# Six loads of the modulation rows move from the input projection to the output projection, and the shift row is finished one chunk later

## Chip, cores and metric

The kernel runs on one core of a Trainium2 chip. The metric is the device time of one execution in microseconds (us). Before the change the median of three runs is 2752.85 us (2752.37 to 2753.55).

## What is computed

Two transformer blocks over 256 tokens of width 2048. What matters here is the first one's modulation: a conditioning vector `c` is multiplied with a 2048 x 12288 matrix, and the result is cut into six rows of 2048.

```python
mod = c_act @ w_ada[l] + b_ada[l]
sh_m, sc_m, gt_m, sh_f, sc_f, gt_f = jnp.split(mod[:, None, :], N_MOD, axis=-1)
h = rmsnorm(x, pre_mix_norm[l]) * (1.0 + sc_m) + sh_m
proj = h @ w_in[l]
...
y = jnp.concatenate([o_hg, o_gdn], axis=-1) @ w_out[l]
x = x + gt_m * rmsnorm(y, post_mix_norm[l])
h = rmsnorm(x, pre_ffn_norm[l]) * (1.0 + sc_f) + sh_f
y = jnp.square(jax.nn.relu(h @ w_ff1[l])) @ w_ff2[l]
x = x + gt_f * rmsnorm(y, post_ffn_norm[l])
```

`gt_m`, `sh_f` and `sc_f` are needed only after the output projection (`@ w_out`), `gt_f` at the end of the block.

## The kernel before

**Units, pairs and chunks.** Every large product is a list of chunks. A chunk is 1024 columns of a weight matrix with all rows of the contraction, which are taken 128 at a time: a *unit*. For one unit ScalarE (ACT) copies the weights to a rounded high part (L424), VectorE (DVE) subtracts that to get a low part (L437), and TensorE (PE) runs twelve matmuls of 512 columns (L475 to L477). Four units may be prepared ahead of the one in work. Weights arrive two units at a time: one DMA of 1 MiB, a *pair*, issued by SyncE (SP, L363) into a ring of four buffers. A load waits until the one four places earlier in the list has been used, so the ring holds whatever the next four loads of the list are. In a chunk of 16 units the pairs are numbered 0 to 7.

**Loads of the modulation rows.** `w_ada` is streamed through the same ring. A chunk's table `ada` names the pairs after which such a load stands in the list (`ada_after`, `load_of`). Each is again 1 MiB: 256 rows of the matrix by half a modulation row of 1024 columns, named by half row (0 to 7) and row pair (0 to 7). DVE uses it after the low part of the pair's second unit, in two steps of 128x1024 (`ada_step`, L455) which add into `MOD`. Half rows 0 and 1 are `gt_m`, 2 and 3 are the shift row `sh_f`; the scale row `sc_f` comes as 16 loads of whole rows after pair 1 of the output projection's first chunk (`mid`), and half rows 6 and 7 are `gt_f`. `ada_used` counts the steps.

**Stages around the change.** The input projection has a short first chunk and six whole ones, at 145 to 460 us of the profile. Its six whole chunks carry all 32 loads of half rows 0 to 3. The output projection (`mix1`, two chunks, *A* and *B* below) starts its units at once, but PE first works off the recurrent mixers (to about 628 us) in a hook of chunk A. From 630 to 732 us PE runs the 32 units of A and B.

**Summing a row.** The steps leave partial sums on each of the 128 partitions. `pe_mod_sum` (L1944) adds them up: eight matmuls with a table of ones into banks 4 to 7 (L1951), then one instruction copies the row back, for `gt_m` on DVE (`dve_mod0`, L2045), for the shift row on ACT (`act_mod1`, L2049), for the scale row on DVE (`dve_mod2`, L2054). All three stand in chunk A, before its units 9, 11 and 13. `dve_mod0` also waits for two rows of 2048 gains, which GpSimd (POOL) loads.

**The order on the engines.** Each engine takes its instructions strictly in order. DVE's list is, unit after unit: low part, the two steps of a modulation load if one stands after this pair, an evacuation of the chunk before, and the hook of the unit two places back. In chunk B that evacuation stands at unit 2: ACT squares a bank, which serves as scratch banks 4 and 5 (L696), DVE multiplies it with `gt_m` (L569), and that frees the bank for PE's first matmul of chunk B.

**POOL's loads.** Once PE has turned the second half of the mixers' output (before unit 7 of chunk A), `pool_norm_ffn1` issues, without waiting in between, two rows spread over all partitions (1 MiB each), the stored memory rows (2 MiB), `x` (2 MiB) and two small ones (L1934 to L1937, L1836). They go through POOL's queue (q0), SP's loads through q1, both on the same 16 DMA engines.

Of the kernel before, what the change touches and what calls it, by code (L numbers as in the profile page):

```python
# [20 lines left out]
KT = D // 128  # L21
# [14 lines left out]
UW = 1024  # L36
# [14 lines left out]
class Chunk:  # L51
# [16 lines left out]
    def ada_after(self, j):  # L68


        return self.mid * (j == 1) if self.mid else int(bool(self.ada) and j in self.ada)

# [9 lines left out]
def number(segments, first_loads, mod_sums, first_out):  # L82
# [5 lines left out]
    ada = 0  # L88
    for iters, chunks in segments:
        for i in range(iters):  # L90
            for c in chunks:
                now = dict(u=u, n=n, ada=ada, done=list(done), signals=list(signals), prev=(prev or {}).get("end"))
                for k in range(0, c.kn, 2):
                    u += min(2, c.kn - k)
                    rel[n] = ("lo", u)
                    n += 1
                    for _ in c.fill if k // 2 == FILL_AFTER else ():
                        native += 1
                        rel[n] = ("native", native)
                        n += 1  # L100
                    for _ in range(c.ada_after(k // 2)):
                        ada += 1 if c.mid else 2
                        rel[n] = ("ada", ada)
                        n += 1
# [57 lines left out]
def block_pair(nc, a, out, stop=None):  # L162

    with ExitStack() as ctx:
# [117 lines left out]
        for n, j in enumerate((6, 7, 0, 1, 2, 3)):  # L282
            for x in ((1, 2, 3, 5, 7), (1, 2, 3, 5, 6, 7))[n >= 4]:
                in_ada.setdefault(j, {})[x] = divmod(sum(len(y) for y in in_ada.values()), 8)
# [11 lines left out]
                          for r0, kn, ph in ((0, 10, "w_out_ab"), (1280, 6, "w_out_c")) for h in range(2)])],  # L296
# [9 lines left out]
                           (1, down2(5, phase="hid2_last", lhs=second))]  # L306
        stages["ffn1"][-1][1][1].phase = "ffn1_tail"
        stages["co"][0][1][1].phase = "co_tail"
        stages["mix2"][0][1][-1].phase = "mix2_tail"
# [29 lines left out]
        if stop != "in":  # L339
            segs[in_segs][1][0].mid = KT  # L340
            segs[in_segs][1][1].ada = mod_loads(6, 0, 1, 3, 5, 7)
        RELEASE, TAIL = number(segs, FIRST_LOADS, DVE_SUMS, ("copy", P, 4 * UW, 0))


# [8 lines left out]
        def sp_chunk(sp, c, i):  # L353
# [12 lines left out]
            for k in range(0, c.kn, 2):  # L366
# [24 lines left out]
                for x in range(c.ada_after(k // 2)):  # L391
                    if c.mid:
                        load(RAW[:, n % RAWN, :, :].rearrange("p j n -> p (j n)"),
                             a["w_ada"][x * 128:x * 128 + 128, 4 * D:5 * D])
                        continue
                    half_row, q = c.ada[k // 2]
                    x0 = 2 * D + half_row * UW
                    load(RAW[:, n % RAWN, :, :], a["w_ada"][q * 256:q * 256 + 256, x0:x0 + UW].rearrange(
                        "(j p) n -> p j n", p=128))
# [30 lines left out]
        def dve_chunk(dve, c, i, hooks, evac):  # L430

            for k in range(c.kn):
# [6 lines left out]
                if c.ada and k % 2 == 1 and k // 2 in c.ada:  # L439
# [4 lines left out]
                    for j in range(2):  # L444
                        ada_step(dve, acc, RAW[:, m % RAWN, j, :], 2 * pair + j,
                                 c.at["ada"] + 2 * sum(c.ada_after(x) for x in range(k // 2)) + j)
                if k == c.dve_evac:
# [95 lines left out]
        def act_evac(act, c, i):  # L543
# [15 lines left out]
            for b, t, h, w, count, (sem, value), col in out_banks(c, i, ("post",)):  # L559
                act.wait_ge(sem, value)  # L560
                act.wait_ge(S("mod_copied"), 3)
                act_square(act, "post_mix", b + 4 * (col // UW), PS[:, b, 0:w], PARTS["post_mix"][:, t, col // 512 + h:col // 512 + h + 1])
# [1076 lines left out]
        MIX1 = next(c for _, cs in segs for c in cs if c.phase == "mix1")  # L1639
        ADA_IN = 4 * KT  # L1640
        MIX_LOAD = MIX1.fill_load(len(KEY_FILL))
# [300 lines left out]

        def pe_mod_sum(pe, row, steps):

            pe.wait_ge(S("ada_used"), steps)
            if row:
                pe.wait_ge(S("mod_copied"), row)
            else:
# [84 lines left out]
        def pe_mod2(pe):  # L2033
            pe_mod_sum(pe, 2, ADA_IN + KT)

        def pe_mod0(pe):
            pe_mod_sum(pe, 0, ADA_IN)

        def pe_mod1(pe):
            pe_mod_sum(pe, 1, ADA_IN)  # L2040

# [5 lines left out]
        def act_mod1(act):  # L2047
            act.wait_ge(S("mod_summed"), 2)
            act.activation(MOD[:, 1, :], bank_cols(4, 4), ACT.Copy).then_inc(S("mod_copied"), 1)  # L2049

        def dve_mod2(dve):
            dve.wait_ge(S("mod_summed"), 3)
            dve.wait_ge(S("masks_in"), 48)
# [3 lines left out]
        def residual_ffn1(dve, link):  # L2057
            dve.wait_ge(S("x2_in"), 16)
            dve_residual(dve, link, "post_mix", Y)

# [87 lines left out]
        def pe_ffn1_tail(pe):  # L2148
            pe_mod_sum(pe, 3, ADA_IN + 3 * KT)

# [835 lines left out]
        def wait_hidden(pe, c, i):  # L2986
            if c.w is a["w_ff2"]:
                wait_hid(pe, c, i)
            else:
# [11 lines left out]
                  ("in1_last", dict(pe=[None] * 10 + [pe_in1_last])),  # L3001
                  ("mix1", dict(pe=tile_waits("mix1", (0, pe_mix1), (7, pe_gdn_split), (9, pe_mod0), (11, pe_mod1), (13, pe_mod2)),
                                act=[None, act_mix1] + [None] * 4 + [act_gdn_split] + [None] * 4 + [act_mod1],
                                dve=[None, dve_mix1, dve_gdn_scale, dve_gdn_gate] + [None] * 2 + [dve_gdn_split] + [None] * 2 +
                                [dve_mod0] + [None] * 3 + [dve_mod2])),
                  ("norm_ffn1", norm_ffn1),
# [135 lines left out]
```

## Time and profile before

| | us |
|---|---|
| median of three runs | 2752.85 |
| the profiled execution | 2751.32 |
| its span, first to last instruction | 2749.5 |
| PE busy | 2663.8 (97%) |
| DVE busy | 1785.1 (65%) |
| ACT busy | 1225.0 (45%) |

The profile is one execution; all stretches below are its times from the start of the span. The rest of the execution's own time, 1.8 us, lies outside the span. A matmul's row says 0.39 us, but such matmuls are pipelined and start about 0.227 us apart, so a unit of twelve takes 2.72 us, and a gap in PE's work is read from the starts and from the idle time in brackets behind a row. A DMA's time to landing counts from its issue on the queue to its completion.

### The profile page before, as it was taken

What the parts mean: (1) busy time and instruction counts of PE and PEld (TensorE: products, weight loads), DVE (VectorE), ACT (ScalarE), POOL (GpSimd) and SP (SyncE); (2) the same over time, 40 slices, a digit from 0 to 9 for tenths busy, and PEclk for the clock granted to TensorE, in tenths of its full rate; (3) what the DMA queues carried; (4) which work ended last, traced back from release to release, by engine and by line L of the source; (5) the groups of instructions that cost most, each with busy time, mean ns of one, the idle gap of its engine ahead of it and who ended that gap; (6) DMA issues with size and microseconds to landing.
All of it is one profiled execution on the core that took longest, in us unless ns stands there. A gap on an engine that the chain in (4) does not pass through costs nothing.

```text
span 2749.5 us, 32675 instructions
## 1 busy us (share of the span) xinstructions
PE 2663.8 (97%) x12618; PEld 2163.5 (79%) x12618; DVE 1785.1 (65%) x2178; ACT 1225.0 (45%) x1572; POOL 69.3 (3%) x92
## 2 busy tenths in 40 slices
PE   5899999899999999999999999999999999999998
PEld 3478887687888888888887777788888888888896
DVE  7887677995785555555577355667665565656576
ACT  2155645343444444444344355544654434353443
POOL 1000000001000000000000100000000000000000
PEclk9999999999999999999999999999999999999999
DMA  9988887345595555555574544444455555555553
GB/s 376 370 289 273 297 303 267 138 178 212 200 365 186 187 191 187 183 189 191 184 290 162 192 154 146 139 160 161 161 199 184 191 188 188 183 186 180 199 173 118
DMA packets 166944, 571.73 MB, mean 208 GB/s; under 512 B 9993, under 2 KB 30648, under 8 KB 162609
## 3 DMA queue, kind: packets, MB, share of 16 engines
q1 hardware_dynamic: 161936, 544.25, 57.3%
q0 software_dynamic: 4720, 25.57, 2.5%
q8 instruction: 74, 1.21, 0.2%
q10 hardware_dynamic: 176, 0.40, 0.0%
q14 instruction: 38, 0.30, 0.0%
HBM read 562.58 MB, written 7.60 MB: 207 GB/s over the span
## 4 chain that ended last, share of the span: by engine, by line
PE 61%; issue 28%; DVE 7%; DMA 2%; ACT 2%; POOL 0%; SPq 0%; DVEq 0%; POOLq 0%; ACTq 0%
PE banks L475 17%; PE banks L477 17%; PE banks L476 17%; DMA raw_weights<-in_w_ada 2%; PE banks L592 1%; DVE mod_in L1019 1%; PE banks L932 1%; ACT weights_high L424 1%; DVE proj L1231 1%; DVE weights_low L437 1%; PE banks L893 1%; PE banks L1951 0%; DVE proj L1215 0%; DMA first_weights<-in_w_in 0%; PE banks L1153 0%
## 5 line engine op out<-in xcount | busy, mean ns | idle before, releaser
L437 DVE TENSOR_TENSOR weights_low<-raw_weights,weights_high 128x1024 fp32r<-128x1024 f32 (+2 forms) x814 | 967.3, 1197 | 732.4 <-ACT weights_high L424 725.0
L424 ACT ACTIVATE weights_high<-raw_weights 128x1024 fp32r<-128x1024 f32 (+2 forms) x814 | 838.8, 1037 | 930.7 <-PE banks L477 889.4
L475 PE MATMUL banks<-weights_high,lhs_high 128*128 128x512 f32 (+1 forms) x2264 | 899.1, 397 | 7.8 <-DVE lhs_low L605 2.2
L477 PE MATMUL banks<-weights_high,lhs_low 128*128 128x512 f32 (+1 forms) x2264 | 882.1, 390 | 0.0
L476 PE MATMUL banks<-weights_low,lhs_high 128*128 128x512 f32 (+1 forms) x2264 | 880.6, 389 | 0.0
L475 PEld LDWEIGHTS banks<-weights_high,lhs_high 128*128 128x128 f32 x2264 | 426.6, 188 | 101.0 <-issue 8.6
L477 PEld LDWEIGHTS banks<-weights_high,lhs_low 128*128 128x128 f32 x2264 | 426.0, 188 | 88.4
L476 PEld LDWEIGHTS banks<-weights_low,lhs_high 128*128 128x128 f32 x2264 | 427.0, 189 | 82.4 <-issue 1.2
L475 PE MATMUL banks<-weights_high,hid_high 128*128 128x512 f32 x768 | 300.8, 392 | 3.0 <-DVE y_rows L574 1.7
L477 PE MATMUL banks<-weights_high,hid_low 128*128 128x512 f32 x768 | 299.2, 390 | 0.0
L476 PE MATMUL banks<-weights_low,hid_high 128*128 128x512 f32 x768 | 299.1, 389 | 0.0
L475 PEld LDWEIGHTS banks<-weights_high,hid_high 128*128 128x128 f32 x768 | 144.2, 188 | 37.2 <-DVE y_rows L574 4.3
L477 PEld LDWEIGHTS banks<-weights_high,hid_low 128*128 128x128 f32 x768 | 144.2, 188 | 30.1
L476 PEld LDWEIGHTS banks<-weights_low,hid_high 128*128 128x128 f32 x768 | 144.2, 188 | 29.3
L455 DVE SCALAR_TENSOR_TENSOR modulation<-raw_weights,columns,modulation 128x1024 f32<-128x1024 f32 (+1 forms) x112 | 160.7, 1434 | 2.6
L1019 DVE SCALAR_TENSOR_TENSOR mod_in<-raw_weights,columns,mod_in 128x512 f32<-128x512 f32 (+1 forms) x150 | 95.5, 645 | 12.3 <-DMA raw_weights<-in_w_ada 7.0
L932 PE MATMUL banks<-first_weights,x_turned 128*128 128x512 f32 x192 | 90.1, 630 | 7.3 <-ACT x_turned L971 6.3
L932 PEld LDWEIGHTS banks<-first_weights,x_turned 128*128 128x128 f32 x192 | 38.3, 202 | 55.3 <-issue 48.7
L2902 ACT ACTIVATE modulation<-modulation 128x512 f32<-128x512 f32 (+1 forms) x22 | 13.7, 623 | 105.6 <-DVE modulation L2929 105.6
L475 PE MATMUL banks<-weights_high,proj_turned 128*128 128x512 f32 x128 | 51.6, 404 | 2.9 <-DVE proj_turned L2530 1.3
L476 PE MATMUL banks<-weights_low,proj_turned 128*128 128x512 f32 x128 | 51.0, 398 | 0.0
L477 PE MATMUL banks<-weights_high,proj_turned 128*128 128x512 f32 x128 | 50.0, 391 | 0.0
(429 smaller groups left out, 2070.0 us busy)
## 6 DMA issues: line engine op xcount, KB each, us to landing
raw_weights<-in_w_ff SPq DMA_DIRECT2D x128, 1024.0 KB, 4.9
raw_weights<-in_w_ada SPq DMA_DIRECT2D x96, 1024.0 KB, 6.9
raw_weights<-in_w_in SPq DMA_DIRECT2D x96, 1024.0 KB, 5.4
raw_weights<-in_w_up SPq DMA_DIRECT2D x80, 1024.0 KB, 5.0
raw_weights<-in_w_down SPq DMA_DIRECT2D x42, 1024.0 KB, 5.0
raw_weights<-in_w_out SPq DMA_DIRECT2D x32, 1024.0 KB, 5.1
first_weights<-in_w_in SPq DMA_DIRECT2D x16, 768.0 KB, 11.9
raw_weights<-in_w_up SPq DMA_DIRECT2D x16, 384.0 KB, 3.8
```

Of the source, the lines that this page charges most:

```text
L424: act.activation(WHI[:, u % SPN, 0:c.width], raw_unit(c, n, k), ACT.Copy).then_inc(S("high_made"), 1)
L437: dve.tensor_tensor(WLO[:, u % SPN, 0:c.width], raw_unit(c, n, k), WHI[:, u % SPN, 0:c.width].bitcast(F32), ALU.subtract).then_inc(S("low_ ...
L455: dve.scalar_tensor_tensor(out=acc, in0=row, scalar=COLS[:, 112 + kt:113 + kt], in1=acc, op0=ALU.mult, op1=ALU.add).then_inc(S("ada_used"), 1)
L475: nc.tensor.matmul(o, x, hi, start=(k == 0), stop=False)
L476: nc.tensor.matmul(o, x, lo, start=False, stop=False)
L477: mm = nc.tensor.matmul(o, y, hi, start=False, stop=(k == c.kn - 1))
L592: tr = nc.tensor.transpose(bank[:, k, 128 * t:128 * t + 128], rows[:, t, c0:c0 + 128], IDENT)
L893: mm = nc.tensor.matmul(PS[:, 6 + t, 0:256], x[:, 128 * t:128 * t + 128], w, start=(k == 0), stop=(k == KT - 1))
L932: mm = nc.tensor.matmul(PS[:, bank, :], XTURN[:, k, 128 * t:128 * t + 128], raw[:, 512 * h:512 * h + 512], start=(k == 0), stop=(k == KT - 1))
L1019: ins = dve.scalar_tensor_tensor(out=acc, in0=row, scalar=c, in1=acc, op0=ALU.mult, op1=ALU.add)
L1231: dve.copy_predicated(self.at[:, t, :].rearrange("p (h n) -> p h n", h=H), mask, self.slot(t).rearrange("p (h n) -> p h n", h=H)).then_inc ...
L2902: act.activation(dst[:, 2 * q:2 * q + nk, :], GT[:, 2 * q:2 * q + nk, :], func).then_inc(S(done), 1)
```

## The change

Six of the 32 loads leave the input projection: its six whole chunks now carry 4, 4, 4, 4, 5 and 5 loads in place of 5, 5, 5, 5, 6 and 6, and half of half row 3 is missing at its end. Four of the six follow pairs 4 to 7 of chunk A, two follow pairs 1 and 2 of chunk B, whose own four loads of `gt_f` move from pairs 1, 3, 5, 7 to 3, 5, 6, 7. The shift row is so complete only in chunk B: its sum on PE and its copy on ACT move there, to unit 10. The scale row's sum moves from unit 13 of A to unit 12 and becomes the second. The waits on the counts follow.

```diff
     def ada_after(self, j):
-        return self.mid * (j == 1) if self.mid else int(bool(self.ada) and j in self.ada)
+        return self.mid * (j == 1) + int(bool(self.ada) and j in self.ada)
...
         for n, j in enumerate((6, 7, 0, 1, 2, 3)):
-            for x in ((1, 2, 3, 5, 7), (1, 2, 3, 5, 6, 7))[n >= 4]:
+            for x in ((1, 3, 5, 7), (1, 2, 4, 5, 7))[n >= 4]:
                 in_ada.setdefault(j, {})[x] = divmod(sum(len(y) for y in in_ada.values()), 8)
...
+        stages["mix1"][0][1][1].phase = "mix1_end"
...
             segs[in_segs][1][0].mid = KT
-            segs[in_segs][1][1].ada = mod_loads(6, 0, 1, 3, 5, 7)
+            segs[in_segs][1][0].ada = {4: (3, 2), 5: (3, 3), 6: (3, 4), 7: (3, 5)}
+            segs[in_segs][1][1].ada = {1: (3, 6), 2: (3, 7), **mod_loads(6, 0, 3, 5, 6, 7)}
...
                 act.wait_ge(sem, value)
-                act.wait_ge(S("mod_copied"), 3)
+                act.wait_ge(S("mod_copied"), 2 + col // UW)
                 act_square(act, "post_mix", b + 4 * (col // UW), ...
...
-        ADA_IN = 4 * KT
+        ADA_IN = 52
...
         def pe_mod2(pe):
-            pe_mod_sum(pe, 2, ADA_IN + KT)
+            pe_mod_sum(pe, 2, ADA_IN + KT, 1)
         def pe_mod0(pe):
-            pe_mod_sum(pe, 0, ADA_IN)
+            pe_mod_sum(pe, 0, 2 * KT, 0)
         def pe_mod1(pe):
-            pe_mod_sum(pe, 1, ADA_IN)
+            pe.wait_ge(S("squares_summed"), SQUARES_BEFORE["post_mix"] + 4)
+            pe_mod_sum(pe, 1, 5 * KT, 2)
...
         def residual_ffn1(dve, link):
             dve.wait_ge(S("x2_in"), 16)
+            dve.wait_ge(S("mod_copied"), 3)
...
-                  ("mix1", dict(pe=tile_waits("mix1", (0, pe_mix1), (7, pe_gdn_split), (9, pe_mod0), (11, pe_mod1), (13, pe_mod2)),
-                                act=[None, act_mix1] + [None] * 4 + [act_gdn_split] + [None] * 4 + [act_mod1],
+                  ("mix1", dict(pe=tile_waits("mix1", (0, pe_mix1), (7, pe_gdn_split), (9, pe_mod0), (12, pe_mod2)),
+                                act=[None, act_mix1] + [None] * 4 + [act_gdn_split],
                                 dve=[None, dve_mix1, dve_gdn_scale, dve_gdn_gate] + [None] * 2 + [dve_gdn_split] + [None] * 2 +
-                                [dve_mod0] + [None] * 3 + [dve_mod2])),
+                                [dve_mod0] + [None] * 2 + [dve_mod2])),
+                  ("mix1_end", dict(pe=[None] * 10 + [pe_mod1], act=[None] * 10 + [act_mod1])),
```

Two places show what this does to the order. The first is SP's list of loads from the scale row on; `in_w_out` are the pairs of the output projection, `in_w_ada` 128x2x1024 the half-row loads. Before:

```order
111 L363 DMA raw_weights<-in_w_ada 128x2048 x16
112 L363 DMA raw_weights<-in_w_out 128x2x1024 x8
113 L363 DMA raw_weights<-in_w_ada 128x2x1024
114 L363 DMA raw_weights<-in_w_out 128x2x1024 x2
115 L363 DMA raw_weights<-in_w_ada 128x2x1024
```

With the change:

```order
99 L365 DMA raw_weights<-in_w_ada 128x2048 x16
100 L365 DMA raw_weights<-in_w_out 128x2x1024 x3
101 L365 DMA raw_weights<-in_w_ada 128x2x1024
102 L365 DMA raw_weights<-in_w_out 128x2x1024
103 L365 DMA raw_weights<-in_w_ada 128x2x1024
104 L365 DMA raw_weights<-in_w_out 128x2x1024
105 L365 DMA raw_weights<-in_w_ada 128x2x1024
106 L365 DMA raw_weights<-in_w_out 128x2x1024
107 L365 DMA raw_weights<-in_w_ada 128x2x1024
108 L365 DMA raw_weights<-in_w_out 128x2x1024 x2
109 L365 DMA raw_weights<-in_w_ada 128x2x1024
110 L365 DMA raw_weights<-in_w_out 128x2x1024
```

The eight pairs (2 to 7 of chunk A, 0 and 1 of chunk B) stood in one run; now a half-row load stands behind each of pairs 4 to 7.

The second is DVE's list in chunk A from unit 9 on, to the evacuation in chunk B. Before, from the low parts of units 9 to 11:

```order
306 L437 TENSOR_TENSOR weights_low<-raw_weights,weights_high 128x1024 x3
307 L2045 TENSOR_TENSOR modulation<-banks,vec 128x2048
308 L437 TENSOR_TENSOR weights_low<-raw_weights,weights_high 128x1024 x4
309 L2054 SCALAR_TENSOR_TENSOR modulation<-banks,hid_rows 128x2048
310 L437 TENSOR_TENSOR weights_low<-raw_weights,weights_high 128x1024 x3
311 L569 TENSOR_TENSOR y_rows<-banks,modulation 128x512 x4
```

With the change, from the steps behind unit 9:

```order
295 L457 SCALAR_TENSOR_TENSOR modulation<-raw_weights,columns,modulation 128x1024 x2
296 L439 TENSOR_TENSOR weights_low<-raw_weights,weights_high 128x1024 x2
297 L457 SCALAR_TENSOR_TENSOR modulation<-raw_weights,columns,modulation 128x1024 x2
298 L2048 TENSOR_TENSOR modulation<-banks,vec 128x2048
299 L439 TENSOR_TENSOR weights_low<-raw_weights,weights_high 128x1024 x2
300 L457 SCALAR_TENSOR_TENSOR modulation<-raw_weights,columns,modulation 128x1024 x2
301 L439 TENSOR_TENSOR weights_low<-raw_weights,weights_high 128x1024
302 L2057 SCALAR_TENSOR_TENSOR modulation<-banks,hid_rows 128x2048
303 L439 TENSOR_TENSOR weights_low<-raw_weights,weights_high 128x1024
304 L457 SCALAR_TENSOR_TENSOR modulation<-raw_weights,columns,modulation 128x1024 x2
305 L439 TENSOR_TENSOR weights_low<-raw_weights,weights_high 128x1024 x3
306 L571 TENSOR_TENSOR y_rows<-banks,modulation 128x512 x4
```

The low parts of units 10 to 15 and the row copies now stand between pairs of steps, each of which needs its own load to have landed.

## Rows read from the trace of the kernel before

**Rows 1.** Page, part 1 and the second row of part 2.

```profile
PE 2663.8 (97%) x12618; PEld 2163.5 (79%) x12618; DVE 1785.1 (65%) x2178; ACT 1225.0 (45%) x1572; POOL 69.3 (3%) x92
```

**Rows 2.** Stretches of the input projection; columns as the first row says.

```profile
core 0: us, PE busy (x) PEld busy (x) DVE busy (x) ACT busy (x) POOL busy (x), PEclk, DMA share, GB/s
...
200.00:320.00 120.00, 120.00 (x590) 99.69 (x589) 90.68 (x108) 78.98 (x99) 2.64 (x3) 1.00 0.84 295
335.00:459.00 124.00, 124.00 (x567) 103.14 (x566) 91.94 (x80) 52.86 (x57) 1.81 (x1) 1.00 0.87 304
```

**Rows 3.** PE's waits from 145 to 461 us: total us, times, longest.

```profile
PE banks L877 <- ACT proj L556: 0.9, 1, 0.9
PE banks L475 <- ACT proj L556: 0.4, 1, 0.4
```

**Rows 4.** More stretches: slow clock in the input projection, and around waits of PE.

```profile
321.00:324.50 3.50, 3.50 (x11) 2.76 (x11) 0.47 (x1) 0.00 (x0) 0.00 (x0) 0.52 1.01 360
331.40:334.80 3.40, 3.40 (x11) 2.82 (x11) 0.27 (x1) 0.27 (x1) 0.00 (x0) 0.50 1.02 357
...
1553.30:1556.80 3.50, 3.50 (x10) 2.74 (x9) 0.00 (x0) 0.20 (x1) 0.61 (x2) 0.51 0.99 380
466.00:474.00 8.00, 6.34 (x34) 4.08 (x33) 7.08 (x23) 7.17 (x11) 0.00 (x0) 1.00 0.41 148
```

**Rows 5.** PE in order of time: the row sums of chunk A; start us, us, instruction.

```profile
658.56 3.59 PE L1951 MATMUL banks<-modulation,tables 128*128 128x512 f32 x8
661.59 0.79 PE L475 MATMUL banks<-weights_high,lhs_high 128*128 128x512 f32 x1
...
667.45 3.59 PE L1951 MATMUL banks<-modulation,tables 128*128 128x512 f32 x8
670.48 0.79 PE L475 MATMUL banks<-weights_high,lhs_high 128*128 128x512 f32 x1
```

**Rows 6.** PE in order of time: first matmul of chunk B; idle before it in brackets.

```profile
688.55 0.47 PE L475 MATMUL banks<-weights_high,lhs_high 128*128 128x512 f32 x1 [0.44 <-DVE y_rows L569]
```

**Rows 7.** SP's issues in order of time, 644 to 692 us.

```profile
644.99 13.98 SPq L363 DMA_DIRECT2D raw_weights<-in_w_out  x4
668.06 0.37 SPq L363 DMA_DIRECT2D raw_weights<-in_w_ada  x1
676.33 9.15 SPq L363 DMA_DIRECT2D raw_weights<-in_w_out  x2
```

**Rows 8.** DMA issues 653.8 to 657.5 us: KB each, us to landing.

```profile
memory_here<-memory_turned POOLq DMA_DIRECT2D x1, 2048.0 KB, 14.8
x_rows<-in_x POOLq DMA_DIRECT2D x1, 2048.0 KB, 22.5
...
hid_rows<-in_pre_ffn_norm POOLq DMA_DIRECT2D x1, 1024.0 KB, 9.0
raw_weights<-in_w_out SPq DMA_DIRECT2D x1, 1024.0 KB, 15.5
```

**Rows 9.** DMA issue at 658.6 us.

```profile
raw_weights<-in_w_out SPq DMA_DIRECT2D x1, 1024.0 KB, 21.7
```

**Rows 10.** DMA issue at 668.1 us.

```profile
raw_weights<-in_w_ada SPq DMA_DIRECT2D x1, 1024.0 KB, 15.4
```

**Rows 11.** DMA queues from 670 to 672 us: packets, MB, share of the engines.

```profile
q1 hardware_dynamic: 66, 0.24, 30.6%
q0 software_dynamic: 65, 0.53, 66.0%
```

**Rows 12.** DVE in order of time, 655 to 692 us.

```profile
655.09 3.50 DVE L437 TENSOR_TENSOR weights_low<-raw_weights,weights_high 128x1024 fp32r<-128x1024 f32 x3
663.47 2.29 DVE L2045 TENSOR_TENSOR modulation<-banks,vec 128x2048 f32<-128x2048 f32 x1 [4.89 <-DMA hid_rows<-in_pre_ffn_norm]
665.68 2.35 DVE L437 TENSOR_TENSOR weights_low<-raw_weights,weights_high 128x1024 fp32r<-128x1024 f32 x2
...
687.72 2.48 DVE L569 TENSOR_TENSOR y_rows<-banks,modulation 128x512 f32<-128x512 f32 x4
...
691.57 2.60 DVE L455 SCALAR_TENSOR_TENSOR modulation<-raw_weights,columns,modulation 128x1024 f32<-128x1024 f32 x2
```

**Rows 13.** ACT in order of time: high parts of chunk B while PE never waits.

```profile
694.37 1.06 ACT L424 ACTIVATE weights_high<-raw_weights 128x1024 fp32r<-128x1024 f32 x1 [1.66 <-PE banks L477]
697.09 1.06 ACT L424 ACTIVATE weights_high<-raw_weights 128x1024 fp32r<-128x1024 f32 x1 [1.66 <-PE banks L477]
```

**Rows 14.** PE in order of time: the wait ahead of the slow clock at 1553 us.

```profile
1552.06 0.91 PE L2316 MATMUL banks<-modulation 33*128 33x384 f32 x2 [2.05 <-ACT modulation L2456]
```

More of the change, by code:

```diff
@@ L101, in number @@
                     for _ in range(c.ada_after(k // 2)):
-                        ada += 1 if c.mid else 2
+                        ada += 1 if c.mid and k // 2 == 1 else 2
                         rel[n] = ("ada", ada)
@@ L391, in sp_chunk @@
                 for x in range(c.ada_after(k // 2)):
-                    if c.mid:
+                    if c.mid and k // 2 == 1:
                         load(RAW[:, n % RAWN, :, :].rearrange("p j n -> p (j n)"),
@@ L445, in dve_chunk @@
                         ada_step(dve, acc, RAW[:, m % RAWN, j, :], 2 * pair + j,
-                                 c.at["ada"] + 2 * sum(c.ada_after(x) for x in range(k // 2)) + j)
+                                 c.at["ada"] + 2 * sum(c.ada_after(x) for x in range(k // 2)) - (c.mid or 0) + j)
                 if k == c.dve_evac:
@@ L1941, in pool_norm_ffn1, with pe_mod_sum @@
             pool_store_values(pool, 0)
-        def pe_mod_sum(pe, row, steps):
+        def pe_mod_sum(pe, row, steps, copied):
             pe.wait_ge(S("ada_used"), steps)
-            if row:
-                pe.wait_ge(S("mod_copied"), row)
+            if copied:
+                pe.wait_ge(S("mod_copied"), copied)
             else:
@@ L2047, in act_mod1 @@
         def act_mod1(act):
-            act.wait_ge(S("mod_summed"), 2)
+            act.wait_ge(S("mod_summed"), 3)
             act.activation(MOD[:, 1, :], bank_cols(4, 4), ACT.Copy).then_inc(S("mod_copied"), 1)
         def dve_mod2(dve):
-            dve.wait_ge(S("mod_summed"), 3)
+            dve.wait_ge(S("mod_summed"), 2)
             dve.wait_ge(S("masks_in"), 48)
@@ L2148, in pe_ffn1_tail @@
         def pe_ffn1_tail(pe):
-            pe_mod_sum(pe, 3, ADA_IN + 3 * KT)
+            pe_mod_sum(pe, 3, 7 * KT, 3)
         def act_ffn1_tail(act):
```

## The prediction

> **What bounds the kernel.** The page's busy times come first: PE works 97% of the span [rows 1], so a change gains only where PE stands still, and costs wherever it makes PE stand still. The table by stretches then shows the stage from which loads are taken: between 200 and 320 us PE is busy 120.00 of 120.00 us, between 335 and 459 us 124.00 of 124.00 [rows 2], although the DMA engines are at 0.84 to 0.87. The list of PE's waits names 1.3 us in all from 145 to 461 us, both behind an evacuation by ACT and neither behind a load [rows 3]. The unit's pace is read from ACT's high parts, which follow PE's releases 2.72 us apart [rows 13]. So the input projection is bound by PE, and DVE and DMA lie beside it. In the output projection the order in time of PE, SP, DVE and the landings must be read together, because there POOL's loads come in. I count times as in the trace of before, and call the pairs of chunk A W5, W6, W7, those of chunk B V0, V1, and the four half-row loads of chunk A G1 to G4.
>
> **The input projection: 0 us.** It loses six loads of 1 MiB, and twelve steps at 1.3 us on DVE (two are 2.60 us [rows 12]). Both stood beside a PE that never waited for them. If this cover were gone, 12 x 1.3 = 15.6 us of DVE time would be the most to save; with PE busy throughout, the bound above is its 1.3 us of waits [rows 3]. Two stretches run at a granted clock of 0.52 and 0.50 [rows 4], 1.2 in place of 2.4 GHz, behind short matmuls; they cost 0.5 x (3.5 + 3.4) = 3.5 us, but the change touches nothing in front of them. I take 0, ends +1 and -4.8.
>
> **The row sums: moved, not saved.** The shift row's sum holds PE from 667.45 to 670.48 us, and the first matmul behind it takes 0.4 us longer than usual [rows 5]: 3.4 us. Before it stands in chunk A, afterwards in chunk B, so it is in the total both times. Its copy on ACT, and the waits put around it (the first four squares and the steps of chunk B's first two loads), end many units before PE's unit 10 of B; ACT, blocked on the sum behind its high part 12, has then prepared what PE needs next. I cost these waits at 0; the cover is the four prepared units, about 8 us (three of 2.72).
>
> **Chunk A: G1 to G4 take places in the ring.** Up to 656 us all goes as before: the ring then holds W4, G1, W5, G2 instead of W4 to W7. From there the loads meet POOL's. Before, SP issued V0 at 656.3 and V1 at 658.6 us as the ring came free [rows 7]; they took 15.5 and 21.7 us to land [rows 8, 9], so at 671.8 and 680.3. The next load, issued at 668.1, took 15.4 [rows 10] and landed at 683.5. The cause is in the same rows: POOL's memory rows and `x` (14.8 and 22.5 us [rows 8]) share the engines. Between 670 and 672 us the queues move 66 and 65 packets, but 0.24 against 0.53 MB [rows 11]: SP's queue gets a packet for each of POOL's, and a third of the bytes, as long as POOL's queue is full. Before, nothing suffered, since W6 and W7 were in the ring already.
>
> Afterwards the same places of SP's queue, issued at the same low parts, carry W6 and G3, then W7 and G4. So W6 lands at 671.8, G3 at 680.3, W7 at 683.5 us. Step by step:
> - PE without the shift row's sum passes units 9 to 11 and the scale row's sum by 673.2 (661.6 + 3 x 2.72 + 0.4 + 3.0). Unit 12 needs W6: high part 1.06 [rows 13], low part 1.15 (three take 3.50 [rows 12]), so 674.1: 0.9 us of waiting.
> - DVE does the low part of 13 and meets the steps of G3, which can't begin before 680.3; they take 2.6 us [rows 12]. W7 landed at 683.5, its high part ends at 684.5, the low part of unit 14 at 685.8. PE has finished unit 13 at 679.7 and waits 6.1 us.
> - DVE goes on without a gap: scale row 2.2 (as the `gt_m` row [rows 12]), low part 15 1.2, steps of G4 2.6, three low parts of chunk B 3.5: 695.3 us. Only then comes the evacuation that frees PE's first bank. Before, it began at 687.72 [rows 12] and PE's chunk B at 688.55 [rows 6], 0.83 us later; so afterwards chunk B begins at 696.1. V1, issued when G3 is used (682.9), lands at about 691, in time for this chain.
>
> Chunk B thus begins 7.5 us later and has the sum of 3.4 us still in it: **+10.9 us**. In chunk B DMA and DVE have caught up; each engine's pace is that of the input projection with modulation loads behind successive pairs, where PE never waited [rows 2]. The norm and the feed-forward follow directly on PE's end and move along.
>
> **The clock behind the new wait.** Before, PE waited 2.05 us at 1552 us [rows 14], behind narrow matmuls, and the granted clock was then 0.51 for a stretch of 3.5 us [rows 4], which costs 0.5 x 3.5 = 1.7 us. The new waits are 6.1 us, and some 4 us before chunk B. A slow stretch behind the first is hidden, since DVE sets the beginning of chunk B; one behind the second costs. Bounds 0 and 2 x 1.7; I take 1.7, since the new wait is longer than that of the row. The Trainium skill ("TensorE: Matmul & The Clock Gate", on the clock gate) says likewise that idling brings the slow clock back.
>
> **Sum.** 0 + 10.9 + 1.7 = 12.6 us. On the profiled execution's 2751.3 that is 2763.9; the median of the runs lies 1.5 us above that execution, which gives 2765.4, and I forecast **2765 us**. Bounds of the terms: from +4 (the waits half as long) to +17 (both slow stretches, and a further wait in chunk B).
>
> **Rivals.**
> - *Not slower: SP's queue catches up.* With three or four loads outstanding instead of two, SP could draw a larger part of the engines. The point from which it decides: G3 landed by about 668 and W7 by about 671 us. Then DVE's list from 663.5 us (row copy 2.2, two low parts, G3, low part, scale row, low part, G4, three low parts) ends near 684 us, as chunk A does on PE (673.2 + 4 x 2.72 = 684.1), and the price is 0: 2752.9 us. For it: SP's queue is merely shared, and DVE has room. Against: SP's queue never ran empty in this stretch before either, and still got 0.24 MB in 2 us [rows 11]; the landings are those of a full queue. The Trainium skill ("DMA: Bandwidth & Descriptors", section on queues, rings and completion order) states that an engine serves its queue rows in turn, a packet each. The 66 and 65 packets agree with it; by that rule more loads in one queue gain no larger part, and this rival gets 0.12 instead of an even chance.
> - *Half the price.* POOL's loads end earlier, or the waits overlap: chunk B begins 3 us earlier than worked out and the clock stays up: +6 to +8, 2760 us. 0.1.
> - *No slow clock:* +10.9, 2763.7 us. 0.2. For it: from 466 to 474 us PE was busy only 6.34 of 8.00 us, and the granted clock was 1.00 [rows 4].
> - *Worse:* a further wait in chunk B, where G loads follow pairs 1 and 2 at once, +14 to +17: 2768 us. 0.08.
> - *Faster.* Fewer loads in the input projection move its two slow stretches or end its waits: -4.8 at most, 2748 us, and the ring's trouble would have to stay away as well. 0.02 for more than 0.2%.
>
> **How the numbers follow.** The forecast itself has 0.48. About 0.2% (5.5 us) is what a measurement of this kernel can tell from no change. Slower by more: 0.48 + 0.2 + 0.08 + 0.1 = 0.86; within it 0.12; faster 0.02. The range 2757 to 2770 takes in all the slower cases and their bounds, and leaves out the other two, 0.14, and a little of the tails.
>
> **What would show it.** In the profile of the changed kernel: the input projection as before, PE without waits on loads; SP's loads issued between 656 and 664 us with 15 to 23 us to landing; DVE idle some 5 us before the steps of a G load near 680, released by a DMA; a PE wait of about 6 us behind a low part near 680 to 686, one of 3 to 4 us behind the evacuation near 692 to 696; the first matmul of chunk B at about 696 us, a slow-clock stretch behind it, and all later stages shifted by one amount. The prediction is wrong if W7 lands before 678 us, or if PE passes from A to B before 690.

## The result, and the profile after

| | before | after |
|---|---|---|
| median of six runs, us | 2752.89 | 2765.03 |
| lowest to highest, us | 2752.37 to 2753.55 | 2763.66 to 2766.93 |
| the profiled execution, us | 2751.32 | 2764.93 |
| its span, us | 2749.5 | 2763.1 |

The ratio is 1.0045, with a 95% interval of 1.0035 to 1.0055: the changed kernel is slower by 12.1 us, and the forecast was 2765. Lines are those of the changed kernel, two higher than before; those of an experiment are its own kernel's.

The page's busy times after the change answer to [rows 1]:

```profile
PE 2669.6 (97%) x12618; PEld 2166.2 (78%) x12618; DVE 1785.2 (65%) x2178; ACT 1224.7 (44%) x1572; POOL 69.3 (3%) x92
```

Every engine runs as many instructions as before, and only PE is busy longer, by 5.8 us: in the slow stretches its rows say 0.63 us for a matmul that takes 0.39 otherwise. The stretches of the input projection, and three at a low granted clock (columns as in [rows 2]):

```profile
200.00:320.00 120.00, 120.00 (x591) 99.66 (x588) 85.86 (x103) 78.91 (x99) 2.64 (x3) 1.00 0.82 278
335.00:459.00 124.00, 124.00 (x566) 103.08 (x566) 86.76 (x76) 52.64 (x56) 1.81 (x1) 1.00 0.82 285
683.30:690.10 6.80, 4.45 (x11) 3.51 (x12) 5.78 (x5) 3.68 (x4) 0.00 (x0) 0.50 0.89 342
697.00:700.30 3.30, 3.30 (x9) 2.62 (x8) 3.27 (x4) 0.47 (x1) 0.00 (x0) 0.50 0.78 226
1564.00:1570.70 6.70, 6.35 (x13) 4.30 (x14) 0.00 (x0) 1.17 (x3) 1.61 (x3) 0.50 0.73 245
```

DVE lost 4.8 and 5.2 us of work in the first two, the DMA engines 0.02 and 0.05 of their share, and PE was busy all the time, as in [rows 2]. Nothing was gained there: the `gt_m` row's sum starts at 658.77 us, where it started at 658.56 before [rows 5]. PE's waits from 655 to 750 us show where the time went:

```profile
PE banks L477 <- DVE weights_low L439: 6.1, 1, 6.1
PE banks L477 <- DVE y_rows L571: 2.1, 1, 2.1
PE banks L895 <- DMA raw_weights<-in_w_ckv: 0.3, 1, 0.3
```

The first two are the waits of the forecast, in front of unit 14 of chunk A and of chunk B. SP's issues at 656.5, 659.1, 661.3 and 663.8 us (W6, G3, W7, G4), each with its time to landing, and the queues from 670 to 672 us:

```profile
raw_weights<-in_w_out SPq DMA_DIRECT2D x1, 1024.0 KB, 14.8
...
raw_weights<-in_w_ada SPq DMA_DIRECT2D x1, 1024.0 KB, 20.9
...
raw_weights<-in_w_out SPq DMA_DIRECT2D x1, 1024.0 KB, 21.8
...
raw_weights<-in_w_ada SPq DMA_DIRECT2D x1, 1024.0 KB, 21.9
...
q0 software_dynamic: 63, 0.52, 65.6%
q1 hardware_dynamic: 65, 0.23, 29.6%
```

The four land at 671.3, 680.0, 683.1 and 685.7 us. With more loads outstanding SP's queue still gets a packet for each of POOL's and 0.23 of 0.75 MB, as in [rows 11]. The Trainium skill ("DMA: Bandwidth & Descriptors", section on queues, rings and completion order) gives the rule, an engine serving its queue rows in turn by packets; 65 against 63 packets agree with it.

DVE in order of time, then ACT, then PE:

```profile
663.74 2.28 DVE L2048 TENSOR_TENSOR modulation<-banks,vec 128x2048 f32<-128x2048 f32 x1
672.47 2.36 DVE L439 TENSOR_TENSOR weights_low<-raw_weights,weights_high 128x1024 fp32r<-128x1024 f32 x2 [6.45 <-ACT weights_high L426]
680.04 2.60 DVE L457 SCALAR_TENSOR_TENSOR modulation<-raw_weights,columns,modulation 128x1024 f32<-128x1024 f32 x2 [5.21 <-DMA raw_weights<-in_w_ada]
684.28 1.23 DVE L439 TENSOR_TENSOR weights_low<-raw_weights,weights_high 128x1024 fp32r<-128x1024 f32 x1 [1.64 <-ACT weights_high L426]
685.42 2.28 DVE L2057 SCALAR_TENSOR_TENSOR modulation<-banks,hid_rows 128x2048 f32<-128x2048 f32 x1
...
688.76 2.60 DVE L457 SCALAR_TENSOR_TENSOR modulation<-raw_weights,columns,modulation 128x1024 f32<-128x1024 f32 x2
691.27 3.49 DVE L439 TENSOR_TENSOR weights_low<-raw_weights,weights_high 128x1024 fp32r<-128x1024 f32 x3
694.68 2.47 DVE L571 TENSOR_TENSOR y_rows<-banks,modulation 128x512 f32<-128x512 f32 x4
```

```profile
671.38 2.01 ACT L426 ACTIVATE weights_high<-raw_weights 128x1024 fp32r<-128x1024 f32 x2 [14.01 <-DMA raw_weights<-in_w_out]
683.19 2.00 ACT L426 ACTIVATE weights_high<-raw_weights 128x1024 fp32r<-128x1024 f32 x2 [9.80 <-DMA raw_weights<-in_w_out]
```

```profile
658.77 3.59 PE L1953 MATMUL banks<-modulation,tables 128*128 128x512 f32 x8
...
670.38 3.59 PE L1953 MATMUL banks<-modulation,tables 128*128 128x512 f32 x8
673.84 0.47 PE L477 MATMUL banks<-weights_high,lhs_high 128*128 128x512 f32 x1
...
685.65 0.76 PE L477 MATMUL banks<-weights_high,lhs_high 128*128 128x512 f32 x1 [6.13 <-DVE weights_low L439]
...
693.05 0.39 PE L479 MATMUL banks<-weights_high,lhs_low 128*128 128x512 f32 x1
695.51 0.47 PE L477 MATMUL banks<-weights_high,lhs_high 128*128 128x512 f32 x1 [2.06 <-DVE y_rows L571]
...
724.43 3.59 PE L1953 MATMUL banks<-modulation,tables 128*128 128x512 f32 x8
...
744.66 3.69 PE L895 MATMUL banks<-raw_weights,memory_here 128*128 128x256 f32 x16 [0.30 <-DMA raw_weights<-in_w_ckv]
```

DVE stands idle 5.21 us until G3 has landed; ACT takes up W7 the moment it lands, at 683.19; from then to the evacuation at 694.68 DVE has no gap but 1.64 us. The shift row's sum stands in chunk B at 724.43. The last row is the first matmul of the norm's product, which follows chunk B. In the kernel before it is this one:

```profile
732.19 13.97 PE L893 MATMUL banks<-raw_weights,memory_here 128*128 128x256 f32 x64
```

From the start of the `gt_m` row's sum to this matmul PE needs 732.19 - 658.56 = 73.63 us before [rows 5] and 744.66 - 658.77 = 85.89 after: **12.26 us more, as much as the medians differ (12.1)**. This distance is used below as *the stretch*. It leaves out what an execution gains or loses earlier and later: the spans of the two profiled executions differ by 13.6 us, and of the other 1.3 us, 0.2 lie before it and the rest near 1564 us, where the slow stretch shown above is 6.7 us long and was 3.5 before [rows 4].

### The profile page after: what moved, and what is told of

Read it like the earlier page. It is cut to its first block, busy times and chain, and to the rows that moved or that the text cites. A ratio compares the mean times of both kernels' runs of the same rounds, so it can differ in the third digit from the quotient of the medians.

```text
span 2763.1 us, 32675 instructions
## 1 busy us (share of the span) xinstructions
PE 2669.6 (97%) x12618; PEld 2166.2 (78%) x12618; DVE 1785.2 (65%) x2178; ACT 1224.7 (44%) x1572; POOL 69.3 (3%) x92
## 4 chain that ended last, share of the span: by engine, by line
PE 60%; issue 28%; DVE 7%; DMA 3%; ACT 2%; POOL 0%; SPq 0%; DVEq 0%; POOLq 0%; ACTq 0%
PE banks L477 17%; PE banks L479 16%; PE banks L478 16%; DMA raw_weights<-in_w_ada 2%; PE banks L594 1%; DVE mod_in L1021 1%; PE banks L934 1%; PE banks L895 1%; ACT weights_high L426 1%; DMA raw_weights<-in_w_out 1%; DVE weights_low L439 1%; DVE modulation L457 1%; DVE proj L1233 1%; DVE proj L1217 0%; DMA first_weights<-in_w_in 0%
## 5 line engine op out<-in xcount | busy, mean ns | idle before, releaser
L1021 DVE SCALAR_TENSOR_TENSOR mod_in<-raw_weights,columns,mod_in 128x512 f32<-128x512 f32 (+1 forms) x150 | 95.5, 644 | 12.2 <-DMA raw_weights<-in_w_ada 6.8
```

Source lines behind the costliest of these rows:

```text
L1021: ins = dve.scalar_tensor_tensor(out=acc, in0=row, scalar=c, in1=acc, op0=ALU.mult, op1=ALU.add)
```

## The experiments

All times are medians; ratios are to runs of the kernel before on the same chip, whose medians were 2752.87 (e1 to e4), 2752.77 (e5 to e7) and 2752.45 us (e8 and e9).

| experiment | median, us | ratio, 95% interval | the stretch, us |
|---|---|---|---|
| before | 2752.89 | | 73.63 |
| after | 2765.03 | 1.0045 (1.0035 to 1.0055) | +12.26 |
| e3, only the sums moved | 2752.92 | 0.9999 (0.9989 to 1.0009) | -0.04 |
| e4, six loads left out | 2753.06 | 1.0001 (0.9992 to 1.0011) | -0.03 |
| e1, POOL's loads in pieces | 2762.71 | 1.0037 (1.0024 to 1.0050) | +7.30 |
| e2, the same in the kernel before | 2756.37 | 1.0009 (1.0000 to 1.0019) | -0.04 |
| e5, two loads in A, one behind pair 0 of B | 2762.03 | 1.0033 (1.0020 to 1.0045) | +6.61 |
| e6, none in A | 2755.82 | 1.0011 (1.0002 to 1.0021) | -0.01 |
| e7, POOL's pieces earlier | 2759.39 | 1.0023 (1.0013 to 1.0032) | +3.80 |
| e9, none in A, seven loads in B | 2752.57 | 1.0002 (0.9993 to 1.0011) | +0.36 |
| e8, none in A, eight loads in B | 2755.83 | 1.0012 (1.0003 to 1.0021) | +3.07 |

**e3: the kernel before, with only the sums moved.** The shift row's sum and copy go to unit 10 of B, the scale row's to unit 12 of A; all loads stay.

```diff
...
-... (9, pe_mod0), (11, pe_mod1), (13, pe_mod2)),
+... (9, pe_mod0), (12, pe_mod2)),
...
+("mix1_end", dict(pe=[None] * 10 + [pe_mod1], act=[None] * 10 + [act_mod1])),
...
```

> The kernel before with only the sum and the copy of the shift row moved to chunk B and the scale row's sum one unit earlier; all loads stay. Theory: PE runs the same instructions, and the waits put around the sum are met long before, so 2752.9 within 1 us. Rival (the sum's new place costs a part of the 12 us): 2756 or more.

2752.92 us, and the stretch is the same. The sums' new places and the waits around them cost nothing.

**e4: the kernel before without the six loads.**

```diff
-            for x in ((1, 2, 3, 5, 7), (1, 2, 3, 5, 6, 7))[n >= 4]:
+            for x in ((1, 3, 5, 7), (1, 2, 4, 5, 7))[n >= 4]:
...
-        ADA_IN = 4 * KT
+        ADA_IN = 52
```

> The kernel before with the input projection's 26 loads in their new places and the other six loads and their twelve steps left out altogether (the shift row lacks six of its sixteen parts). Theory: the input projection is bound by PE, so six loads and twelve steps less are worth nothing: 2752.9 within 1.5 us. Rival (the relief is worth something that the output projection then eats up): 2750 or less.

2753.06 us. The stretch from 200 to 320 us:

```profile
200.00:320.00 120.00, 120.00 (x590) 99.65 (x589) 85.86 (x103) 78.92 (x99) 2.64 (x3) 1.00 0.81 279
```

DVE is freed of 4.8 us and PE is as busy as ever: relieving the input projection of the six loads is worth nothing by itself.

**e1: the change, with POOL's memory rows and `x` in eight pieces of 512 KiB**, each issued behind a unit of chunk B instead of all at 655 us.

```diff
-            pool.dma_start(MEM_HERE[:, :, :].rearrange("p k t -> p (k t)"), a["memory_turned"]).then_inc(S("mem_in"), 16)
-            pool.dma_start(X[:, :, :], a["x"].rearrange("(t p) d -> p t d", p=128)).then_inc(S("x2_in"), 16)
+            last = stages["mix1"][0][1][1].at["u"]
+            for n, unit in enumerate((0, 1, 3, 5, 7, 9, 11, 13)):
+                pool.wait_ge(S("unit_used"), last + unit + 1)
...
```

> The changed kernel, but POOL's stored memory rows and x (2 MiB each) are issued in pieces of 512 KiB during chunk B instead of all at once before unit 7 of chunk A; every load and step of the change stays where it is. Theory (POOL's loads make SP's loads late): SP's loads issued at 656 to 664 us land in about 5 to 8 us, PE passes chunk A without the wait of 6 us and without a slow-clock stretch, chunk B begins near 685 us with the sum of 3.4 us still in it, and the median falls by most of the 12 us, to 2753 to 2757 (the rest for pieces that now meet chunk B's loads). Rival (the 10 us of steps on DVE, in order with the low parts, are too much for chunk A by themselves): the wait at unit 14 and at the start of chunk B stays, 2762 to 2766.

2762.71 us, far above what was expected. PE's waits from 640 to 745 us, and the four loads issued from 656 to 664 us:

```profile
PE banks L895 <- DMA raw_weights<-in_w_ckv: 7.2, 1, 7.2
PE banks L477 <- DVE weights_low L439: 1.0, 2, 0.5
PE banks L477 <- DVE y_rows L571: 0.4, 1, 0.4
```

```profile
raw_weights<-in_w_out SPq DMA_DIRECT2D x2, 1024.0 KB, 9.7
raw_weights<-in_w_ada SPq DMA_DIRECT2D x2, 1024.0 KB, 9.7
```

The mechanism is as the theory has it: without the two big transfers the same loads land in 9.7 us instead of 15 to 22 (5 to 8 were expected; POOL's two rows of 1 MiB are still beside them), the wait of 6.1 us is gone, and chunk B's wait is that of [rows 6]. But the transfers still have to be made. Their last pieces now meet the first loads of the norm's product. The one issued at 724.8 us:

```profile
raw_weights<-in_w_ckv SPq DMA_DIRECT2D x1, 1024.0 KB, 14.4
```

PE waits for it 7.2 us behind chunk B, and from 737.6 to 744.4 us the granted clock is 0.50: the norm's product takes 16.50 us instead of 13.97. With these 2.5 us, the stretch's 7.3 make the 9.8 by which the medians differ. The price was not removed but moved; the expectation had overlooked the next loads in SP's queue.

**e2: the kernel before, with the same pieces.** Same edit, in the kernel before.

> The kernel before with the same pacing of POOL's loads, to price the pacing alone. Theory: before, POOL's loads hid behind the full ring, so nothing is gained, and the pieces fit between chunk B's loads: 2752 to 2756. Rival (POOL's burst cost the kernel before something too): 2749 or less.

2756.37 us, just above what was expected. The stretch is unchanged; behind it PE loses 1.6 us in the norm, most of it in one wait of 2.3 us instead of 1.1. The rest of the 3.5 us was not located; the other delays of this execution lie near 136 us and from 1538 to 1563 us, in stretches of slow clock far from the edit. So these 1.6 us are what the trace shows as the price of spreading out POOL's loads alone. Whether it is more is not shown, and the interval begins at 1.0000.

**e7: as e1, but earlier.** POOL's two small loads go first, and the pieces follow units 0, 1, 2, 4, 6, 8, 10, 11 of B.

```diff
-            for n, unit in enumerate((0, 1, 3, 5, 7, 9, 11, 13)):
+            for n, unit in enumerate((0, 1, 2, 4, 6, 8, 10, 11)):
```

> The run with POOL's loads in pieces, with the two small scattered loads ahead of the pieces and the pieces earlier in chunk B, since the last pieces and the small loads made the first two weight loads of the memory values late there (a wait of 7.2 us after chunk B). All loads and steps of the change stay. Theory: no wait in chunk A, at most 2 us after chunk B: 2752 to 2756. Rival (the change costs its price somewhere whatever POOL does): 2760 or more.

2759.39 us, again above what was expected. PE's waits from 640 to 745 us, and the load issued at 726.0 us:

```profile
PE banks L895 <- DMA raw_weights<-in_w_ckv: 2.9, 1, 2.9
PE banks L477 <- DVE weights_low L439: 1.0, 2, 0.5
PE banks L477 <- DVE y_rows L571: 0.8, 1, 0.8
...
raw_weights<-in_w_ckv SPq DMA_DIRECT2D x1, 1024.0 KB, 10.0
```

The same load, which took 5.0 us before, now takes 10.0 and costs 2.9. Less, but not nothing: from 685 to 733 us the DMA engines' share is 1.00, against 0.77 before and 0.80 after the change. Chunk B has no free place for POOL's 4 MiB. The norm's product takes 15.59 us, again in part at a granted clock of 0.50; with these 1.6 us, the stretch's 3.8 make 5.4 of the 6.6 by which the medians differ.

**e5: two loads in chunk A instead of four**, behind pairs 4 and 5; the other four behind pairs 0 to 3 of B, the four of `gt_f` behind pairs 4 to 7.

```diff
-            segs[in_segs][1][0].ada = {4: (3, 2), 5: (3, 3), 6: (3, 4), 7: (3, 5)}
-            segs[in_segs][1][1].ada = {1: (3, 6), 2: (3, 7), **mod_loads(6, 0, 3, 5, 6, 7)}
+            segs[in_segs][1][0].ada = {4: (3, 2), 5: (3, 3)}
+            segs[in_segs][1][1].ada = {**mod_loads(3, 4, 0, 1, 2, 3), **mod_loads(6, 0, 4, 5, 6, 7)}
```

> The changed kernel with two of the four loads behind chunk A's pairs kept there (pairs 4 and 5) and two moved to chunk B, which carries shift loads behind pairs 0 to 3 and its own behind 4 to 7. Theory (what counts is which loads stand in SP's queue while POOL's burst holds the engines): W6 is still first in the queue and lands at about 671, W7 is now second and lands at about 680 in place of 683, DVE has no steps between units 13 and 14; PE waits about 3 us at unit 14 and chunk B begins near 689.5 in place of 695.5: +4 to +7, 2757 to 2760. Rival (four loads or two make no difference, the wait comes from the moved sum or the ring's two places): 2763 or more. Other rival (linear in the loads moved to A): half of 12, 2759, which does not tell it from the theory; the landing times do.

PE's waits from 640 to 745 us:

```profile
PE banks L477 <- DVE weights_low L439: 3.7, 3, 2.7
PE banks L477 <- DVE y_rows L571: 2.5, 1, 2.5
```

ACT takes up W7 when it lands, and DVE comes to the steps of the load behind pair 0 of B:

```profile
679.73 2.00 ACT L426 ACTIVATE weights_high<-raw_weights 128x1024 fp32r<-128x1024 f32 x2 [6.40 <-DMA raw_weights<-in_w_out]
687.56 2.60 DVE L457 SCALAR_TENSOR_TENSOR modulation<-raw_weights,columns,modulation 128x1024 f32<-128x1024 f32 x2
```

W7 now has the ring's place that G3 had and lands at 679.7 instead of 683.1 us. The wait in front of unit 14 is 2.7 instead of 6.1: shorter by about these 3.4 us. The load behind pair 0 puts its steps where those of G4 stood, so from W7's landing to chunk B's first matmul DVE has the same work as after the change. The stretch is 6.6 us longer, of which 3.2 stand in front of chunk B and 3.4 are the sum. The median, 2762.03 us, lies above what was expected. It is another 2.7 us higher than the stretch says, and 3.0 above the profiled execution (2758.99). Where the other runs lose this was not seen. Four of those five list a mean granted clock of 0.991, the profiled one 0.992; more slow clock would fit, but is not shown.

**e6: none in chunk A.** 28 loads stay in the input projection, four stand behind pairs 1 to 4 of B, and one of `gt_f`, for which B has no place left, goes to the feed-forward's first chunk. The shift row's sum stands at unit 12 of B.

```diff
-            segs[in_segs][1][0].ada = {4: (3, 2), 5: (3, 3), 6: (3, 4), 7: (3, 5)}
-            segs[in_segs][1][1].ada = {1: (3, 6), 2: (3, 7), **mod_loads(6, 0, 3, 5, 6, 7)}
+            segs[in_segs][1][1].ada = {**mod_loads(3, 4, 1, 2, 3, 4), **mod_loads(6, 0, 5, 6, 7)}
...
-... ada=mod_loads(6, 4, 3, 5, 6, 7)
+... ada={**mod_loads(6, 4, 3, 5, 6, 7), 2: (6, 3)}
```

> Four loads instead of six leave the input projection (28 stay there), and all four stand in chunk B, behind pairs 1 to 4; chunk B keeps three loads of its own, the fourth goes to the first chunk of the feed-forward; the shift row's sum stands at unit 12 of B. Nothing stands in chunk A's ring but its pairs, POOL's burst stays as it was. Theory: PE passes A without waits on loads, and B begins as early as before less the sum: 2752 to 2755. Rival (any load moved out of the input projection costs about 2 us where it goes): 2759 or more.

The stretch is as before: chunks A and B are free of new waits. The median, 2755.82 us, is 3.0 us above the kernel before and just above what was expected. What the profiled execution (the slowest of the ten) loses near the edit lies in the feed-forward, where the odd load stands. DVE there, then PE and a stretch at a low granted clock:

```profile
763.33 2.61 DVE L456 SCALAR_TENSOR_TENSOR modulation<-raw_weights,columns,modulation 128x1024 f32<-128x1024 f32 x2 [3.97 <-DMA raw_weights<-in_w_ada]
```

```profile
769.61 0.77 PE L476 MATMUL banks<-weights_high,lhs_high 128*128 128x512 f32 x1 [2.37 <-DVE weights_low L438]
769.20:772.60 3.40, 2.99 (x7) 2.47 (x8) 3.36 (x4) 1.58 (x2) 0.00 (x0) 0.50 1.02 376
```

It is the pattern of chunk A in small: steps that wait for their load hold up the low parts behind them. A new edit had brought a new wait, so the question was asked once more without it.

**e9: none in A, and only three loads moved.** 29 stay, three stand behind pairs 1 to 3 of B, the four of `gt_f` behind pairs 4 to 7. **e8: none in A, four moved.** 28 stay, and all eight pairs of B are followed by a load, pair 0 too.

```diff
...
+            segs[in_segs][1][1].ada = {**mod_loads(3, 5, 1, 2, 3), **mod_loads(6, 0, 4, 5, 6, 7)}    (e9)
...
+            segs[in_segs][1][1].ada = {**mod_loads(3, 4, 0, 1, 2, 3), **mod_loads(6, 0, 4, 5, 6, 7)} (e8)
...
```

> The change with 29 loads left in the input projection, none in chunk A, and three shift-row loads behind pairs 1 to 3 of chunk B, the four of gt_f behind pairs 4 to 7 (seven of eight pairs followed by a load); the sum and copy of the shift row stay in unit 10 of B. Theory (the price of the change is that of the four places in chunk A, where POOL's loads take two thirds of the bytes; loads in chunk B and the moved sum cost nothing): PE without a wait on a load from 630 to 745 us, first matmul of B near 685, first matmul of the norm's product within 0.5 us of before, 2752 to 2754 us. Rival (each load that leaves the input projection costs PE time wherever it lands, about 2 us each): 2757 us or more.

> The change with 28 loads left in the input projection, none in chunk A, and all eight pairs of chunk B followed by a load (four of the shift row, then four of gt_f). The one behind pair 0 takes the ring's place that pair 1 has otherwise, and is issued near 658 us. Theory (landings follow the place in SP's queue while POOL's loads run): that load lands at 680.1, pair 1 at 683.2; DVE's steps end at 682.7, the low part of unit 2 of B at about 685.5, and B's first matmul comes at about 686.3 instead of 685.1: a wait of 1.2 to 2 us in front of B and none elsewhere, 2754 to 2755.5 us, or 2756 to 2757 with a slow-clock stretch behind it. Rival (a load in chunk B is free behind any pair): no wait, 2752 to 2753.5 us.

The first matmul of chunk B in e9; then in e8, with a stretch at a low granted clock and the load behind pair 0:

```profile
687.05 0.47 PE L476 MATMUL banks<-weights_high,lhs_high 128*128 128x512 f32 x1 [0.44 <-DVE y_rows L570]
```

```profile
688.43 0.47 PE L476 MATMUL banks<-weights_high,lhs_high 128*128 128x512 f32 x1 [1.91 <-DVE y_rows L570]
689.50:692.80 3.30, 3.30 (x9) 2.54 (x8) 3.03 (x4) 0.78 (x1) 0.00 (x0) 0.50 0.66 205
...
raw_weights<-in_w_ada SPq DMA_DIRECT2D x1, 1024.0 KB, 21.7
```

Both executions run 1.9 us later than before at the `gt_m` row's sum, so the times themselves don't compare with [rows 6], the waits do. (So does e2's, by 1.8 us, with the input projection of the kernel before. In all three the granted clock is 0.50 or 0.51 for some 3.4 us near 136 us, where it was 1.00 before; these executions, not the edits, lose the time.) e9 costs nothing: three loads taken from the input projection and seven in chunk B, with the sum there, are free within the interval. In e8 the one load behind pair 0 takes a place in SP's queue while POOL's loads run: issued at 660.5 us it takes 21.7 us to land, and pair 1 comes behind it. The wait in front of chunk B is 1.91 instead of 0.44 us, and with the slow stretch behind it (half of 3.3 us) that is 1.47 + 1.65 = 3.1; the stretch says 3.07, the medians 3.4. One load, one place earlier, costs as much as that.

## Why the prediction was right

- **Input projection, 0.** Shown twice: by the stretches after, and by e4, where the relief stands alone.
- **Row sums moved, not saved.** The sum's row is in chunk B at 724.43; e3 gives 0 for the move.
- **Landings.** Forecast 671.8, 680.3 and 683.5 us, measured 671.3, 680.0 and 683.1: the places of SP's queue kept their times, and other loads sat in them. e1 shows that POOL's transfers are the cause: take them out of the stretch, and the loads land in 9.7 us and the wait is gone. The rival in which SP's queue catches up needed G3 by 668; it fails by 12 us.
- **Unit 12, 0.9 us.** Mis-sized: nearly nothing. Its first matmul comes 3.46 us behind the start of the sum (670.38 to 673.84), where it comes 3.03 behind in [rows 5] and then takes 0.4 longer. The high and low parts of W6 were finished earlier than reckoned.
- **Unit 14, 6.1 us.** Measured 6.13.
- **Chunk B's start.** Forecast 7.5 us late, measured 695.51 - 688.55 = 7.0, of which 0.2 was there already at the `gt_m` row's sum: 6.8. DVE's list ran as reckoned, 0.6 us earlier; V1, forecast for 691, landed at 690.8.
- **The second wait, "some 4 us".** Measured 2.06; the prediction's own times leave more than 4. The slow clock from 683.3 to 690.1 lay over units 14 and 15: from the first to the last of their 24 matmuls PE needed 693.05 - 685.65 = 7.4 us, where 23 steps of 0.227 make 5.2. This lengthening by 2.2 took the place of waiting, and DVE's list ended 0.6 earlier. That this stretch costs nothing, since DVE sets the start of B, was in the forecast.
- **The clock behind the second wait, 1.7 us.** 3.3 us at 0.50 (the stretch from 697.0) make 1.65. The size came out, but the reason given for it did not: the wait was to be longer than the one at 1552 us and was as long, and in e5 one of 2.52 us at this place had no slow stretch behind it. That the stretch came was in part luck.
- **Not in the forecast:** 0.30 us of waiting for the first load of the norm's product.

6.8 + 3.4 + 1.65 + 0.3 = 12.2 us, against 12.6 forecast and 12.26 measured. The errors of the terms are below 1 us each and partly cancel. That the median meets the forecast to a tenth of a microsecond is luck, since the six executions alone are 3.3 us apart. Two loads in chunk A with one behind pair 0 of B (e5) cost 6.6 us, one behind pair 0 (e8) 3.1, none in these places (e9) nothing: the price is that of the places ahead of pair 1 of B. A half-row load there puts the pairs behind it at a later place of SP's queue, while POOL's queue is full. No version beat the kernel before; with PE busy 97% of the span and the input projection bound by it, e3, e4 and e9 tie with it.

## What to carry to other kernels

Before a streamed load is moved to a stage with free DMA share, look at what the other queue carries just then, and write the new load into the list of the old issue times: the landing of the load that had a place before was here a forecast, good to half a microsecond, for the load that takes it. Where engines work in order, an extra consumer on DVE delays everything behind it by the landing of its own load, even where the load is small and the engine idle. And a burst on another queue that hurts can't simply be spread out: here its bytes met the next stage's loads (e1, e7).

## What was not expected of the hardware

**The slow clock behind one and the same wait varies.** Near 1552 us PE waits 2.0 to 2.1 us in every one of these kernels [rows 14]. The slow stretch around it was 3.5 us in the execution before [rows 4], 6.7 after the change, and in the profiled execution of e9 there were two:

```profile
1548.70:1552.10 3.40, 3.40 (x9) 2.66 (x9) 0.00 (x0) 0.00 (x0) 0.54 (x1) 0.51 0.94 341
1555.60:1562.40 6.80, 6.29 (x13) 4.24 (x14) 0.00 (x0) 1.33 (x4) 1.83 (x4) 0.50 0.74 243
```

Together they are 10.2 us at half speed. That costs some 3.3 us more than the 3.5 us before, and this execution, with the slow stretch near 136 us besides, took 2756.57 us where the median of its kernel is 2752.57. Of one execution's difference to another's, a few us can be this alone; the stretch of the trace that the edit touches is the safer measure, as the table shows.

**The length of a wait alone does not tell whether a slow stretch follows.** In front of chunk B, 1.91 us of waiting (e8) and 2.06 (after) were followed by 3.3 us at 0.50; 2.52 us in e5 were not. The Trainium skill ("TensorE: Matmul & The Clock Gate", Part 1) states that the number of slow matmuls differs from run to run of the same kernel. The stretches near 1552 us agree, as far as kernels with the same code there can stand for one kernel.
